# A bidirectional RWKV-7 scan: its matrix products spread over four quarters of TensorE, its level matrices made on GpSimd, its wide products made five chunks ahead

## The reference, cut to what matters

```python
def step(S, inp):
    r_t, w_t, k_t, v_t, a_t, b_t = inp
    sa = jnp.einsum('bhij,bhj->bhi', S, a_t)
    S = (S * w_t[:, :, None, :] + sa[..., :, None] * b_t[..., None, :]
         + v_t[..., :, None] * k_t[..., None, :])
    return S, jnp.einsum('bhij,bhj->bhi', S, r_t)
_, ys = lax.scan(step, S0, xs, reverse=reverse)
```

## Time and profile before

| | us |
|---|---|
| median of 3 runs | 2501.82 (2499.22, 2501.82, 2515.18) |
| profiled execution | 2509.72, span 2508.0 |

### The profile page before, as it was taken

How to read it: one execution, slowest core, us unless ns; L and a number is a source line. 1 busy time by engine, 2 the same in 40 slices (tenths; PEclk the granted TensorE clock), 3 DMA queues, 4 the chain that set the end, 5 groups by cost and what they waited for, 6 DMA issues and landing times. The chain is left out here.

```text
span 2508.0 us, 50080 instructions
## 1 busy us (share of the span) xinstructions
PE 2328.4 (93%) x19504; PEld 2035.2 (81%) x19504; DVE 1827.3 (73%) x2480; ACT 1208.3 (48%) x1748; POOL 709.5 (28%) x715
## 2 busy tenths in 40 slices
PE   6899999999996999996989896699999999999997
PEld 4788888888876898986767674699999999999996
DVE  5547888988865676675767677677777777777777
ACT  6355454445522334432335332566565666666656
POOL 2234242433412444454453534011011111101111
PEclk9999999999997999998999998799999999999998
DMA  4335253442537766763647352777777777777777
GB/s 151 85 96 162 86 161 116 137 149 87 172 114 226 210 188 188 192 173 79 234 128 258 111 202 101 301 246 256 264 256 245 237 258 255 251 251 260 264 256 245
DMA packets 294772, 479.74 MB, mean 191 GB/s; under 512 B 142224, under 2 KB 209952, under 8 KB 266832
## 3 DMA queue, kind: packets, MB, share of 16 engines
q1 hardware_dynamic: 275552, 412.52, 50.1%
q0 software_dynamic: 7760, 27.08, 4.8%
q10 hardware_dynamic: 11296, 37.82, 4.6%
HBM read 363.51 MB, written 110.69 MB: 189 GB/s over the span
## 5 line engine op out<-in xcount | busy, mean ns | idle before, releaser
L2751 PE MATMUL bank<-e_xt,e_w_high 128*128 128x384 f32 x1792 | 524.7, 357 | 3.7 <-DVE e_xt L2919 2.1
L2906 DVE TENSOR_TENSOR e_w_low<-e_w,e_w_high 128x2048 fp32r<-128x2048 f32 x192 | 436.2, 2284 | 69.2 <-ACT e_w_high L2807 69.2
L2752 PE MATMUL bank<-e_xt,e_w_low 128*128 128x192 f32 x1792 | 449.1, 251 | 0.0
L2807 ACT ACTIVATE e_w_high<-e_w 128x2048 fp32r<-128x2048 f32 x192 | 366.4, 1908 | 107.8 <-PE bank L2773 79.2
L2752 PEld LDWEIGHTS bank<-e_xt,e_w_low 128*128 128x128 f32 x1792 | 342.2, 191 | 0.6
L2751 PEld LDWEIGHTS bank<-e_xt,e_w_high 128*128 128x128 f32 x1792 | 338.1, 189 | 5.5 <-issue 2.5
L462 PE MATMUL bank<-h_high,w_high 128*128 128x512 f32 x864 | 258.0, 407 | 1.5 <-DVE work L872 1.5
L855 DVE SCALAR_TENSOR_TENSOR work<-work,vec 128x1551 f32<-128x1551 f32 x116 | 243.8, 2102 | 2.4
L465 PE MATMUL bank<-h_low,w_high 128*128 128x512 f32 x864 | 244.8, 391 | 0.0
L468 PE MATMUL bank<-h_high,w_low 128*128 128x512 f32 x864 | 243.7, 390 | 0.0
L2685 POOL DMA_INDIRECT xacc_dram<-e_y,e_put x30 | 47.3, 1576 | 651.9 <-DVE e_y L2941 647.3
(11 more groups left out here) (356 smaller groups left out, 5168.7 us busy)
## 6 DMA issues: line engine op xcount, KB each, us to landing
e_w<-in_ew SPq DMA_DIRECT2D x192, 1024.0 KB, 5.9
features_dram<-work SPq DMA_DIRECT2D x48, 512.0 KB, 3.3
fe<-features_dram SPq DMA_DIRECT2D x24, 1024.0 KB, 8.1
x_w<-in_w_mix SPq DMA_DIRECT2D x48, 512.0 KB, 5.1
w<-in_w_in ACTq DMA_DIRECT2D x35, 512.0 KB, 3.6
ba_tok_dram<-work SPq DMA_DIRECT2D x96, 128.0 KB, 2.2
gates_dram<-work ACTq DMA_DIRECT2D x16, 768.0 KB, 4.5
all<-ba_tok_dram SPq DMA_DIRECT2D x96, 128.0 KB, 3.4
```

Of the source, the lines that this page charges most:

```text
L2751: nc.tensor.matmul(*wide, start=(k == 0), stop=False)
L2752: nc.tensor.matmul(*narrow, start=False, stop=False)
L2807: nc.scalar.activation(w_high[n % RING][:], w[n % RING][:], ACT.Copy).then_inc(w_high_done, 1)
L2906: tt(w_low[n % RING][:], w[n % RING][:], w_high[n % RING][:].bitcast(F32), ALU.subtract)\
```

## The change

What it does, part by part:

- **Quarters.** Direction 1 now reads its weights from one half of the partitions and writes to the other half (`HALF`, `STATE`, `TOKEN`), and the loops over `hp` alternate between the directions. A set of four 64 x 64 matmuls in a row so addresses all four quarters of the array (rows 0-63 or 64-127 by columns 0-63 or 64-127), where before only two were addressed. To undo the swap, ACT copies two halves apart where it copied one tile (`swapped`), and `compact` loads direction 1 by three DMAs where it had one.
- **State.** The two matmuls of 64 weight columns per head become one of 128. `state(i-2)` stands at the head of body i, where `state(i-1)` stood at the end.
- **Products.** `products` is split: `products_wide` (N = 128, G with M or RB) is made `FIRST` = 5 chunks ahead, `products_narrow` and `products_c` four ahead. `ALL` has 6 buffers where it had 5.
- **POOL.** `levels` moves from DVE to POOL, as two small instructions per direction, ahead of `expand`. The convolution's sums move from DVE to POOL (its squares to ACT). `invert` stands in passes of odd i, one chunk further ahead; the last pair isn't halved any more.
- **SP.** `inverses` stands in passes of even i, `tokens` always ahead of `compact`, and `values` moves to ACT's queue. `lower(i+5)` is the last of a pass, `diagonal(i+4)` the first.

The numbers of chunks ahead and of buffers, and the halves:

```diff
-    LEVELS, AHEAD, RING = 2, 4, 5
+    LEVELS, AHEAD, FIRST, RING, RING_ALL, PARTS = 2, 4, 5, 5, 6, 3
...
+        STATE, TOKEN = ROWS, ROWS[::-1]
+        HALF = [ROWS, ROWS[::-1]]
```

`compact(i)`, on SP:

```diff
-                        sp.dma_start(XC[d][i % 2][:].rearrange("p h x c -> p h (x c)"),
-                                     src.rearrange("(h k) (p e) -> (k p) h e", h=HP, p=BASE)).then_inc(l_x[d][i % 2], 16)
+                        if d == 0:
+                            sp.dma_start(XC[d][i % 2][:].rearrange("p h x c -> p h (x c)"), src).then_inc(l_x[d][i % 2], 16)
+                        else:
+                            sp.dma_start(XC[d][i % 2][:, :, 0, :], src[:, :, 0:BASE]).then_inc(l_x[d][i % 2], 16)
+                            for out, r in zip(ROWS, HALF[d]):
+                                sp.dma_start(XC[d][i % 2][out, :, 1, :], src[r, :, BASE:2 * BASE])\
+                                  .then_inc(l_x[d][i % 2], 16)
```

SP's loop:

```diff
-                    if 1 <= i and i + AHEAD - 1 < NCH:
-                        diagonal(i + AHEAD - 1)
-                    if i % 2 == 1 and 3 <= i < NCH - 3:
-                        inverses((i + 1) // 2)
-                    if i % 2 == 0 and i >= 4:
+                    if i + FIRST - 1 < NCH:
+                        diagonal(i + FIRST - 1)
+                    if i % 2 == 0 and 2 <= i < NCH - AHEAD - 2:
+                        features((i + AHEAD + 2) // 2)
+                    if i % 2 == 0 and 2 <= i < NCH - 2:
+                        inverses((i + 2) // 2)
+                    if 1 <= i < NCH - 1:
+                        tokens(i + 1)
+                    if i == 1:
+                        compact(3)
+                    if 3 <= i < NCH - 1:
                         compact(i + 1)
```

`state(d, i)`, on PE:

```diff
                     for h in range(HEADS):
-                        for x, r in enumerate(ROWS):
-                            mm = nc.tensor.matmul(bank[LATE[d]][r, h * HD:(h + 1) * HD], FU[d][:, h, x, :],
-                                                  ST[d][i % 2][:, h, :], start=True, stop=True)
+                        mm = nc.tensor.matmul(bank[LATE[d]][:, h * HD:(h + 1) * HD],
+                                              FU[d][:, h, :, :].rearrange("p x c -> p (x c)"),
+                                              ST[d][i % 2][:, h, :], start=True, stop=True)
```

`level_n(i, n)`, on PE (`level_x`, `solve` and the products likewise):

```diff
                     for hp in L4:
-                        for r in ROWS:
-                            mm = nc.tensor.matmul(t_bank(d)[r, hp, :], NL[d][s][r, n, hp, :], x[d][s][r, hp, 0, :],
-                                                  start=True, stop=True)
+                        for d in DIRS:
+                            for z, r in enumerate(ROWS):
+                                mm = nc.tensor.matmul(t_bank(d)[HALF[d][z], hp, :], NL[d][s][r, n, hp, :],
+                                                      x[d][s][r, hp, 0, :], start=True, stop=True)
```

`products_wide(j)`, new on PE:

```diff
+                    for hp in L4:
+                        for d in DIRS:
+                            c = inner(d, j)
+                            for z, r in enumerate(ROWS):
+                                ar, kb = AR[d][u][r, hp, :, c], KB[d][u][r, hp, :, c]
+                                left, right = (kb[:, 1, :], ar) if d == 0 else (ar[:, 0, :], kb)
+                                mm = nc.tensor.matmul(wide_of(d, j)[HALF[d][z], hp, :], left, right, start=True, stop=True)
```

`body(i)`, on PE (only what stands there now; the lines it replaces are in the code above):

```diff
+                    if i >= 2:
+                        for d in DIRS:
+                            state(d, i - 2)
+                    level_n(i, 0)
                     if post:
+                        solve(i - 1)
+                    level_x(i, 0)
+                    if pre:
+                        products_narrow(i + AHEAD)
+                    if post:
                         full(0, i - 1)
+                    if i + FIRST < NCH:
+                        products_wide(i + FIRST)
+                    level_n(i, 1)
                     if post:
                         full(1, i - 1)
                     if pre:
+                        products_c(i + AHEAD)
+                    level_x(i, 1)
```

`levels(d, i)`, new on POOL, and POOL's loop:

```diff
+                def levels(d, i):
+                    if i >= 2:
+                        pool.wait_ge(m_n[d], (i - 1) * LEVELS)
+                    pool.wait_ge(v_g[d], i + 1)
+                    for n, blocks in enumerate((slice(1, None, 2), slice(2, None))):
+                        part = lambda v: v.rearrange("p h (b c) -> p h b c", c=BASE)[:, :, blocks, :]
+                        level = mk("level", n * HD, HD).unsqueeze(1).to_broadcast([P, HP, HD])
+                        ins = tt(part(NL[d][i % 2][:, n, :, :]), part(ALL[d][i % RING_ALL][:, :, G_[d], :]), part(level),
+                                 ALU.mult)
+                    ins.then_inc(p_n[d], 1)
...
                 for i in range(1, NCH - 1):
                     for d in DIRS:
+                        levels(d, i + 1)
+                    for d in DIRS:
                         expand(d, i + 1)
-                    if i % 2 == 0 and i + 4 < NCH:
-                        invert((i + 2) // 2)
+                    if i % 2 == 1 and i + 3 < NCH:
+                        invert((i + 3) // 2)
+                    conv(i)
```

577 lines of the change are left out of this document (285 added, 292 removed).

## The result

The changed kernel takes **2561.97 us** (median of 4 runs, 2557.19 to 2566.91), the kernel before 2503.29 us beside it (4 runs, 2499.22 to 2515.18): a ratio of 1.0229, 95% interval 1.0194 to 1.0263. It is slower, as forecast, but by 58.7 us and not by 30, and outside the forecast range of 2503 to 2552.

A forecast was written before the change was run, and what follows sets the result against it. Two close bounds: PE at some 15 us per body, the SP-DRAM-POOL loop at 16. The loop's turn grows from 31.98 to 34.7 us; nine turns, start and end give +30 us: 2532 us, range 2503 to 2552.

The forecast's parts named there:

- nine turns: Scan, between the stores of inverses 2 and 11: 34.7 us for each two bodies, up from 31.98.
- Without one body of 15 and some 5 us of waits ... I take 50: Last four bodies and close of the scan: 50 us (45 to 56) instead of 69.5.
- PE has 12.9 us per turn as cover: PE in the turns: 34.7 - 21.8 = 12.9 us of slack covers its part-time lower clock.
- the 10.9 forecast: PE's work per scan body: 7.4 us plus 3.5 for state, 10.9 us, from 15.
- The rule of the Trainium skill: PE: matmuls never start under some 25 ns apart; PE's body would be 13.1 us, rival A left as it is.
- the first step: Scan before: PE bounds at some 15 us per body, the loop through SP, DRAM and POOL at 16.
- rival B: Scan: PE sets a faster pace, SP's own issues next at 26 us per turn; 2442 us; chance 0.13.
- The tokens ahead of `xc`, +2.94 us in the sum: SP's loop: four tokens ahead of the second `compact` lengthen the turn by 2.94 us.
- the additional loads of `xc`, 1.4 us: SP's loop: four more `xc` issues per turn, priced at +1.1 and +0.3 us.
- 5 us sooner: Start of the scan: the store of inverse 2 comes at 838.8 us instead of 843.8.
- PE idle 10 us at the head of odd bodies: Sign of being right: PE waits about 10 us for `x0_` at the head of every odd body.
- PE's busy time down by a quarter or more: Sign of being right: PE's busy time in the scan falls by a quarter or more while the stage lengthens.

The follow-up runs named there:

- 64 columns: Changed kernel, with each head's state product again as two matmuls of 64 weight columns: ratio 1.0157, 2545.6 us.
- The run with PE kept busy: Changed kernel plus unread matmuls: eight ahead of the wait for `x0_` in odd bodies, six ahead of the second `full` group in the last four: ratio 1.0278.
- both bounds eased: Changed kernel with a quarter of each features load from pair five, plus 3 of 14 inversion steps (1.0103) or `xc` ahead of tokens in odd passes (1.0102).
- the short chain: Changed kernel with 64-column state products, features issued by ScalarE, and SP's odd passes ordered `xc`, `gb`, tokens: ratio 1.0143.
- the kernel before with 128 columns: Kernel before, with only each head's two state products made one of 128 weight columns: ratio 1.0084, 2530.0 us.
- the short chain and a quarter: Changed kernel with 64-column state, features on ScalarE, odd passes `xc`, `gb`, tokens, and a quarter of each features load from pair four: ratio 1.0052.

## Why the prediction was right and wrong

**Its ledger.** Against the forecast of the profiled execution: the store of inverse 2 at 844.15 instead of 838.8 us, +5.3; nine turns in 304.8 instead of 312.3, -7.5; from store 11 (1148.91) to body 21 (1163.5) 14.6 instead of 10.3, +4.3; the end 68.5 instead of 50, +18.5. Together +20.6: the scan ends at 1232 and not at 1211. The forecast took the end of the scan before as 1181.5 us, but its last instruction ends at 1183.0, so the scan got 49 us longer, not 50.6. What lies behind it kept its length (1325.0 before, from 1183.0 to 2508.0; 1327.2 after). The rest of the 58.7 us is the executions: the profiled one of before was 6.4 us above its four runs' median, that of after 0.9 below.

**The end: the term that failed.** "Without one body of 15 and some 5 us of waits ... I take 50" was carried over from the kernel before, whose last groups had a clock of 0.93 and state groups of 2.1 to 3.6 us. I had priced the new state for the turns (3.5 us, where waiting covers it) and left it out of the end, where nothing covers it, although the diff puts `state(d, i - 2)` at the head of a body and `level_n`, DVE's addition and `solve` behind it. It is paid there four times, three times at 7.09 us and once at 3.79. With 64 columns the end takes 54.2 us: 14.3 of the 18.5 us are this. The other 4.2 are nearly all the base: the forecast took a body of 15 us off 69.5, but body 20 took 12.4 (1112.02 to 1124.46), and 1.5 us were missing behind 1181.5. With both right, 58.5 us less the 5 of waits gives 53.5, near the 54.2 of 64 columns. The other half of the slip is "PE has 12.9 us per turn as cover" for the lower clock: true in the turns, not behind them. The run with PE kept busy shows the clock as the cause of the 7.09 us.

**The body of PE: right in its parts.** The quarters overlap: `level_n` 0.52 us for both directions. All groups but `full` and `state` take 7.08 us per body instead of 10.93, where 5.2 were forecast at the full clock; at the mean of 0.85 that makes 6.1, and the last us is not accounted for. State: 3.79 us at the full clock against 3.5, 4.48 on average. PE idles 2.8 us per body and not 5: it works 3.1 us more per body than the 10.9 forecast. The rule of the Trainium skill that was weighed (TensorE: Matmul & The Clock Gate, the section on 56 ns and 53.3 ns), no start within some 25 ns of the last, doesn't hold over four quarters: 32 records start within 0.52 us, 16 ns apart on average. The 31 ns that the prediction set beside it is an average too. Record by record, the trace of before has pairs 6 to 7 ns apart and some 52 ns to the next pair, the trace after has fours 5 to 8 ns apart and 38 to 39 ns to the next four. PE's body was not what decided, so this had no part in the miss.

**The loop: right in its number, wrong in its reason.** The turn came to 33.9 us against 34.7, with the expected order of waits in it. But the first step, "PE is the bound at some 15 us per body and the loop at 16", was wrong for the kernel before. With 8 us less in that loop its body shrank by 0.1 us, and 1.6 us more for PE's state groups lengthened it by 1.0. Its loop had slack, which was in full view. Ahead of the keys SP stands 3.1 us per turn until DVE, which follows PE, is done: that wait was PE's pace and not the loop's length, and I took 1.1 of it off. In five of six turns SP didn't wait for the inversion at all. The 3.5 us ahead of `gb` are another thing: there SP waits for G's stores to land, and the changed kernel has 3.3 us of it too. In the changed kernel the loop does bind, but beside it stands a second bound of the same length that I had put at 26 us (rival B: 21.5 of issues at their usual price and two waits for landing). With the inversion out of the way SP issues for 27.6 us of a turn of 34.8, as issues behind 2 MB of features cost more, and stands 7.2 between them. So that two bounds lie a few per cent apart was true of the new kernel, with another second bound. That the sum came within 0.8 us is luck in part: its terms don't add as it took them. The tokens ahead of `xc`, +2.94 us in the sum, gave 0.3 when they were put back, and the additional loads of `xc`, 1.4 us, gave nothing (34.2 for 33.9).

**The start.** "5 us sooner" didn't come: the first store is 2.6 us later than before (787.78 for 785.22) and the next two turns take 28.2 and 28.1 us, not 25.6 and some 28. The longer first turn I didn't isolate. The later first store goes with the wide products of two chunks that now come first on PE, but that is read from the order and not tried.

**Signs.** Stores some 35 us apart: 33.9, held. `level_n` at 0.5: held. State at 1.8 us a group: 1.9 at the full clock, 3.5 at the lower. POOL waiting for `xc` ahead of each inversion: held in the turn shown, 111.2 us in 27 waits in all. PE idle 10 us at the head of odd bodies: failed, from 800 to 1112 us it waits there for `x0_` six times, 18.6 us in all and 6.9 at most. PE's busy time down by a quarter or more: failed, 13.98 us per body from 15.38, 9%; state and the lower clock had filled the rest. What lies outside the scan kept its length: held.

**What stays open.** With both bounds eased the turn is still 30.3 to 31.7 us, more than the 28.4 of the short chain. The run with state behind `level_n` shows that PE's odd body can be in it too, and PE's gaps inside groups (last section) may be; the share of neither was measured. Nor was it told apart whether the features hold SP up by their bytes or by their packets. The 4.3 us between store 11 and body 21 were not looked into further.

## What to carry over

PE was busy 95 to 97% of the stage and was the bound there, however unbroken the row of issues on the queue beside it looked. A wait in such a row which the bound engine releases is slack of the queue, and has to come off before the queue is called a loop of that length; a wait for a landing is not. Before you price a change of order in a steady stage, price its last bodies apart: there the waits that hid a group are gone, PE pauses, its clock drops, and a group with wide weights pays double. And when one cut in a chain gives nothing, cross it with a second one: here cuts worth 0.1 to 0.8 us a turn alone gave 2.3 and 3.6 together.

## What the runs showed of the hardware

- Records over four quarters (64 rows by 64 columns each, N = 64) need half the time of the same records over two: 0.52 us for 32 and not 0.98, 16 ns from start to start on average, 28 ns at the lower clock (0.91 us for 32).
- One product of 128 weight columns with N = 64 in f32 takes 118 ns per record at the full clock (3.79 us / 32) and 222 at the lower (7.09 / 32). The same work as 64 records of 64 columns, in two halves of the columns, takes 33 ns each (2.09 / 64), 55% of the time.
- Issuing a load is not a fixed price: two `gb` took 1.06 us in the kernel before and 4.39 in the short chain with 64 columns, one `xc` 0.55 and 3.63, the dear ones while 2 MB were under way on ScalarE's queue. With the 2 MB ahead on SP's own queue, four `xc` took 6.2 us for 2.5.
- Inside groups of PE the profile has gaps without a wait for another engine. Counting those over 0.4 us between 800 and 1112 us, they sum up to 7.3 us in the kernel before (8 gaps), 24.8 in the changed one (13, the longest 3.4) and 1.8 in the kernel before with 128 columns (one); no record is missing around them, bodies 8 to 17 of the changed kernel have all their 352 or more each. They don't follow the features: with a quarter of these 15.7, with the short chain and a quarter 34.0. They follow the loading of instructions. All 13 gaps of the changed kernel end 1.2 to 1.5 us after a packet of 16 KB on the DMA queue q8 of kind "instruction" has ended; such packets come 6.0 us apart there. Over the profiles of all 18 kernels it is 254 of 256 gaps within 1.1 to 1.7 us. By that PE stood until a block of its own program had come. This is read from the order in time and not tried by a run; why some blocks came late, and what the gaps cost in time, stays open.
